# Two accumulation tables in place of one for the expert outputs of a decoder step, and a final stage in two halves

## The reference

```
scores = sigmoid(h @ router_w)                      # 64 experts, 8 chosen for each token
act    = silu(h @ e_gate) * (h @ e_up) * gates      # for each expert, on its tokens
routed = sum over experts of act @ e_down
x      = x + gate2 * (routed + shared)
y      = x * rsqrt(mean(x * x) + EPS) * final_g     # final norm
```

## Time and profile before

| | |
|---|---|
| median of 3 runs | 1003.78 us (1003.36 to 1004.73) |
| time of the profiled execution | 1004.73 us |
| span of the profiled execution | 1003.0 us, first to last instruction |
| mean granted TensorE clock | 0.976 |
| busy share of the span | PE 91%, DVE 47%, ACT 28%, POOL 17% |
| read from HBM, written | 305.79 MB, 25.90 MB |

### The profile page before, as it was taken

One profiled execution on the slowest core, in us unless ns is written; L12 is line 12 of the kernel. 1 busy time (PEld: TensorE's weight loads), 2 busy tenths in 40 slices (PEclk: granted clock), 3 DMA queues, 4 the chain that ended last, 5 costly groups with the idle time before them and its releaser, 6 DMA issues.

```text
span 1003.0 us, 18411 instructions
## 1 busy us (share of the span) xinstructions
PE 916.1 (91%) x6409; PEld 642.9 (64%) x6409; DVE 468.1 (47%) x1217; ACT 276.0 (28%) x491; POOL 172.8 (17%) x177
## 2 busy tenths in 40 slices
PE   2799999999998999999999999999999988889890
PEld 1599999999997986445555555555555445445440
DVE  1557889899968464422333233323223222222124
ACT  3554444443274220012222212221212111111121
POOL 2000000000000001122222222232222222222120
PEclk9899999999999989999999999999999999999995
DMA  9884558878877169679999999999999999999833
GB/s 329 261 250 144 170 174 288 276 252 299 281 260 245 55 234 368 245 270 341 411 397 398 412 394 398 395 403 384 390 393 381 376 374 364 342 367 358 306 97 101
DMA packets 101761, 305.53 MB, mean 305 GB/s; under 512 B 13379, under 2 KB 53379, under 8 KB 76716
## 3 DMA queue, kind: packets, MB, share of 16 engines
q1 hardware_dynamic: 87275, 281.63, 75.1%
q0 software_dynamic: 13936, 21.79, 8.5%
q10 hardware_dynamic: 499, 1.40, 0.4%
HBM read 305.79 MB, written 25.90 MB: 331 GB/s over the span
## 4 chain that ended last, share of the span: by engine, by line
DMA 45%; PE 44%; DVE 5%; issue 4%; ACT 1%; POOLq 0%; SPq 0%; ACTq 0%; POOL 0%; DVEq 0%
DMA y_even<-mT,scatter_row 30%; PE psum L760 26%; DMA wexp<-in_e_up 12%; PE psum L1031 7%; PE psum L764 3%; PE psum L779 2%; PE psum L1059 2%; PE psum L947 1%; DMA bc<-in_norm_g 1%; DMA xn<-h_table,idx 1%; PE psum L1002 1%; DVE wexp_r L1439 1%; DMA mid<-in_c_prompt 0%; DVE x_sb L1990 0%; PE psum L1064 0%
## 5 line engine op out<-in xcount | busy, mean ns | idle before, releaser
L760 PE MATMUL psum<-xn_r,wexp_r 128*128 128x264 f32 x1024 | 191.6, 287 | 2.2 <-DVE wexp_r L1439 2.2
L1033 PE MATMUL psum<-wexp,mid 128*64 128x256 f32 x720 | 175.4, 387 | 11.5 <-DMA wexp<-in_e_up 11.2
L1034 PE MATMUL psum<-wexp,mid 128*64 128x256 f32 x720 | 175.7, 387 | 0.0
L684 POOL DMA_INDIRECT y_even<-mT,scatter_row x64 | 95.1, 1486 | 399.2 <-ACT mT L1359 174.7
L760 PEld LDWEIGHTS psum<-xn_r,wexp_r 128*128 128x128 f32 x1024 | 160.3, 190 | 3.3 <-DVE wexp_r L1439 2.5
L1031 PE MATMUL psum<-wexp,mid 128*128 128x512 f32 x304 | 140.3, 605 | 9.5 <-DMA wexp<-in_e_up 8.7
L760 PE MATMUL psum<-hT_r,wexp_r 128*128 128x264 f32 x512 | 145.6, 284 | 0.0
L1854 DVE SCALAR_TENSOR_TENSOR hT<-psum,gcol,hT 128x256 f32<-128x256 f32 (+1 forms) x64 | 30.6, 478 | 222.5 <-ACT hT L1352 222.5
L1033 PEld LDWEIGHTS psum<-wexp,mid 128*64 128x64 f32 x720 | 92.8, 137 | 51.8 <-issue 17.8
L1862 DVE COPY mT<-psum 128x512 f32<-128x512 f32 (+1 forms) x64 | 43.9, 685 | 175.9 <-DMA y_even<-mT,scatter_row 102.7
L1439 DVE TENSOR_TENSOR wexp_r<-wexp,wexp_r 128x1024 fp32r<-128x1024 f32 x88 | 106.4, 1218 | 22.5 <-ACT wexp_r L1198 22.4
(11 more groups left out here) (285 smaller groups left out, 1008.1 us busy)
## 6 DMA issues: line engine op xcount, KB each, us to landing
wexp<-in_e_gate SPq DMA_DIRECT2D x64, 1024.0 KB, 8.7
wexp<-in_e_up SPq DMA_DIRECT2D x64, 1024.0 KB, 18.9
wexp<-in_e_down SPq DMA_DIRECT2D x64, 1024.0 KB, 19.1
wexp<-in_w_in SPq DMA_DIRECT2D x32, 1024.0 KB, 6.4
mid<-in_ada_w SPq DMA_DIRECT2D x8, 2048.0 KB, 9.8
wexp<-in_ada_w SPq DMA_DIRECT2D x4, 2048.0 KB, 20.5
wexp<-in_w_branch SPq DMA_DIRECT2D x8, 1024.0 KB, 6.1
wexp<-in_w_out SPq DMA_DIRECT2D x4, 1024.0 KB, 5.8
```

What stands on the lines that cost most here:

```text
L684: g.indirect_dma_start(out=y_even, out_offset=bass.IndirectOffsetOnAxis(ap=scatter_row[0:n, j, :].bitcast(mybir.dt.uint32), axis=0), in_=y ...
L760: last = mm(out, a[x], b[y], start=start and x == y == 0, stop=stop and x == 1)
L1033: mm(psum[HALF:CAP, j % 2, 0:FE], x[:, k, 0:HALF], w[:, k, 0], start=(k == 0), stop=(k == KT - 1), tile_position=(0, HALF))
L1034: last = mm(psum[0:HALF, j % 2, 0:FE], x[:, k, 0:HALF], w[:, k, 1], start=(k == 0), stop=(k == KT - 1), tile_position=(0, 0))
```

## The change

Scatters of even places go to `y_even`, those of odd places to `y_odd`, and each table has a semaphore of its own. A scatter waits only for the previous one into the same table, that is for expert e - 2. The waits of `y_out` and `keep_scatter_row` name the same scatters as before, counted by parity. `y_odd` is filled with zeros as well.

The final stage is in two halves. Once the last even scatter (expert 62) has landed, SP loads `y_even`. DVE multiplies and adds it to all three tiles, now ahead of its `extra_passes`. After all scatters and `extra_passes`, `y_odd` is loaded; DVE takes tiles 0 and 1, and POOL takes the 8 rows of tile 2 with the same two operations. The order in which tiles are finished and stored is 0, 1, 2 in place of 2, 0, 1; only the loads of `y_odd` keep 2, 0, 1. POOL waits for both semaphores before its `extra_passes`, and ACT's table load for the root stands ahead of them.

```diff
-        fin_y = wexp[:, 1, 0:3 * D].rearrange("p (t d) -> p t d", t=3)
+        fin_y = wexp[:, 1, :].rearrange("p (a t d) -> p a t d", a=2, t=3)
...
-            for table in (y_even,):
+            for table in (y_even, y_odd):
...
+            sp.wait_ge(S["down_done"], 2 * (NE - 2))
+            sp.wait_ge(scattered[0], 16 * (NE // 2))
+            for t, (t0, n) in enumerate(TILES):
+                sp.dma_start(fin_y[0:n, 0, t], y_even[t0:t0 + n]).then_inc(S["even_load"], 16)
             sp.wait_ge(S["down_done"], 2 * NE)
             extra_passes(sp, extra)
 
             sp.wait_ge(S["moe_done"], 1)
-            sp.wait_ge(S["scattered"], 16 * NE)
-            for t in FINAL_ORDER:
+            for t in (2, 0, 1):
                 t0, n = TILES[t]
-                sp.dma_start(fin_y[0:n, t], y_even[t0:t0 + n]).then_inc(fin_ld[t], 16)
-            for m, t in enumerate(FINAL_ORDER):
-                t0, n = TILES[t]
-                sp.wait_ge(S["fin_ready"], m + 1)
+                sp.dma_start(fin_y[0:n, 1, t], y_odd[t0:t0 + n]).then_inc(fin_ld[t], 16)
+            for t, (t0, n) in enumerate(TILES):
+                sp.wait_ge(S["fin_ready"], t + 1)
...
-            pool.wait_ge(S["tables_zero"], 2 * 16)
+            pool.wait_ge(S["tables_zero"], 4 * 16)
...
-                need(pool, S["scattered"], 16 * e)
+                need(pool, scattered[j % 2], 16 * (2 * i + j // 2))
...
-                g.indirect_dma_start(out=y_even, out_offset=...
+                g.indirect_dma_start(out=(y_even, y_odd)[j % 2], out_offset=...
...
             scatter(NE // UNROLL - 1, UNROLL - 1)
-
-            def all_scattered():
-                pool.wait_ge(S["scattered"], 16 * NE)
+            pool.wait_ge(scattered[0], 16 * (NE // 2))
+            pool.wait_ge(scattered[1], 16 * (NE // 2))
...
-            extra_passes(pool, extra, all_scattered)
+            extra_passes(pool, extra)
             pool.sem_inc(S["moe_done"], 1)
-            all_scattered()
+
+            t, n = 2, NS
+            pool.wait_ge(fin_ld[t], 16)
+            link(g.tensor_tensor(out=fin_y[0:n, 1, t], in0=fin_y[0:n, 1, t], in1=rows_of(3, t, n, 0, D), op=ALU.mult))
+            pool.wait_ge(S["even_taken"], 3)
+            g.tensor_tensor(out=x_sb[0:n, t, :], in0=x_sb[0:n, t, :], in1=fin_y[0:n, 1, t], op=ALU.add).then_inc(S["fin_samples"], 1)
...
-                need(ac, S["scattered"], 16 * (e - 1))
+                need(ac, scattered[j % 2], 16 * (2 * i + j // 2))
...
+            F(sqrt_first[:], epsc[:], ACT.Sqrt)
             extra_passes(ac, extra)
-            F(sqrt_first[:], epsc[:], ACT.Sqrt)
-            for m, t in enumerate(FINAL_ORDER):
-                n = TILES[t][1]
-                ac.wait_ge(S["fin_red"], m + 1)
+            for t, (t0, n) in enumerate(TILES):
+                if t == 2:
+                    ac.wait_ge(S["fin_samples"], 1)
+                else:
+                    ac.wait_ge(S["fin_red"], t + 1)
...
+            ve.wait_ge(S["even_load"], 3 * 16)
+            for t, (t0, n) in enumerate(TILES):
+                link(V.tensor_tensor(fin_y[0:n, 0, t], fin_y[0:n, 0, t], rows_of(3, t, n, 0, D), ALU.mult))
+                V.tensor_tensor(x_sb[0:n, t, :], x_sb[0:n, t, :], fin_y[0:n, 0, t], ALU.add).then_inc(S["even_taken"], 1)
             extra_passes(ve, extra, shift_small)
 
-            for t in FINAL_ORDER:
+            for t in range(2):
                 n = TILES[t][1]
                 ve.wait_ge(fin_ld[t], 16)
-                link(V.tensor_tensor(fin_y[0:n, t], fin_y[0:n, t], rows_of(3, t, n, 0, D), ALU.mult))
-                V.tensor_tensor(x_sb[0:n, t, :], x_sb[0:n, t, :], fin_y[0:n, t], ALU.add).then_inc(S["fin_red"], 1)
+                link(V.tensor_tensor(fin_y[0:n, 1, t], fin_y[0:n, 1, t], rows_of(3, t, n, 0, D), ALU.mult))
+                ve.wait_ge(S["even_taken"], t + 1)
+                V.tensor_tensor(x_sb[0:n, t, :], x_sb[0:n, t, :], fin_y[0:n, 1, t], ALU.add).then_inc(S["fin_red"], 1)
```

More of the change, by code:

```diff
@@ L57 @@
 MIX_ORDER = (2, 0, 1)
-FINAL_ORDER = (2, 0, 1)
 X2_AT = {t: MIX_JOBS.index((t, 1)) + 1 for t in MIX_ORDER}
@@ L336, in bass_decoder_step @@
         gathered = [sem(f"gathered{b}") for b in range(UNROLL)]
+        scattered = [sem(f"scattered{b}") for b in range(2)]
         gu_full = [sem(f"gu_full{s}") for s in range(UNROLL)]
@@ L683, in scatter @@
                 n = rows_used(i, j)
-                g.indirect_dma_start(out=y_even, out_offset=bass.IndirectOffsetOnAxis(ap=scatter_row[0:n, j, :].bitcast(mybir.dt.uint32), axis=0),
+                g.indirect_dma_start(out=(y_even, y_odd)[j % 2], out_offset=bass.IndirectOffsetOnAxis(ap=scatter_row[0:n, j, :].bitcast(mybir.dt.uint32), axis=0),
                                      in_=y_rows[0:n, j % 2, :], in_offset=None,
-                                     bounds_check=last_token, oob_is_err=False, compute_op=ALU.add).then_inc(S["scattered"], 16)
+                                     bounds_check=last_token, oob_is_err=False, compute_op=ALU.add).then_inc(scattered[j % 2], 16)
             await_full(pool, ("h2T", MIX_ORDER[-1], 1))
@@ L720, in extra @@
                 pool.sem_inc(S["dma_may_go"], 1)
-                g.indirect_dma_start(out=y_even, out_offset=bass.IndirectOffsetOnAxis(ap=idx[:, 0, 0:1].bitcast(mybir.dt.uint32), axis=0),
+                g.indirect_dma_start(out=y_odd, out_offset=bass.IndirectOffsetOnAxis(ap=idx[:, 0, 0:1].bitcast(mybir.dt.uint32), axis=0),
                                      in_=y_rows[:, 0, :], in_offset=None,
@@ L1827, in keep_scatter_row @@
                 ve.wait_ge(S["lst_ready"], e + 1)
-                need(ve, S["scattered"], 16 * (e - 3))
+                need(ve, scattered[j % 2], 16 * (2 * i + j // 2 - 1))
                 n = rows_used(i, j)
@@ L1859, in y_out @@
                 ve.wait_ge(S["down_done"], 2 * e + 2)
-                need(ve, S["scattered"], 16 * (e - 1))
+                need(ve, scattered[j % 2], 16 * (2 * i + j // 2))
                 n = rows_used(i, j)
@@ L1975, in extra @@
                 ve.wait_ge(S["x_sc"], 16 * n + 16)
+            ve.wait_ge(S["even_load"], 3 * 16)
+            for t, (t0, n) in enumerate(TILES):
+                link(V.tensor_tensor(fin_y[0:n, 0, t], fin_y[0:n, 0, t], rows_of(3, t, n, 0, D), ALU.mult))
+                V.tensor_tensor(x_sb[0:n, t, :], x_sb[0:n, t, :], fin_y[0:n, 0, t], ALU.add).then_inc(S["even_taken"], 1)
             extra_passes(ve, extra, shift_small)
[L1980 removed]
+            for t in range(2):
                 n = TILES[t][1]
                 ve.wait_ge(fin_ld[t], 16)
[L1983 to L1984 removed]
+                link(V.tensor_tensor(fin_y[0:n, 1, t], fin_y[0:n, 1, t], rows_of(3, t, n, 0, D), ALU.mult))
+                ve.wait_ge(S["even_taken"], t + 1)
+                V.tensor_tensor(x_sb[0:n, t, :], x_sb[0:n, t, :], fin_y[0:n, 1, t], ALU.add).then_inc(S["fin_red"], 1)
             ve.wait_ge(S["ld_fin"], 16)
[L1986 to L1988 removed]
+            for t, (t0, n) in enumerate(TILES):
+                ve.wait_ge(S["fin_sq"], t + 1)
                 link(V.reciprocal(st[0:n, t, 2:3], st[0:n, t, 1:2]))
```

7 lines of the change are left out of this document (2 added, 5 removed).

## The result

The changed kernel takes 1013.40 us (median of 4 runs, 1012.96 to 1013.97), the kernel before on the same chip 1004.06 us (4 runs, 1003.36 to 1004.73): a ratio of 1.0086, 95% interval 1.0064 to 1.0106. The ratio is taken over all fast executions of the changed kernel, 21 with a median of 1012.68 us, and so is a little less than that of the two medians here. So the change costs 9 to 11 us. The direction of the forecast was right. Its size, 3.6 us, was not, and the time lies above the whole range (1009.0).

What follows compares the result with a forecast made beforehand. The prediction took the slowest DMA engine's backlog of weights to bound the loop. With the loop at 0, the end's sum of +0.2 us and POOL's hold of 3.4 gave 1003.78 + 3.6 = 1007.4 us, range 1001.0 to 1009.0.

Steps and rivals of the forecast that it cites:

- Scatters overlap in the loop: Expert loop: free scatters were put at 0, with ends of 3.5 us gained and 1 us lost.
- The sign of the 3.5 us of PE: Loop: PE regains up to 3.5 us from late gathers, taken as no gain; rival of a faster loop, chance 0.20.
- Zeros, 0: Before the loop: filling y_odd takes SP 9.03 us, from 325.5 to 334.6, all covered; cost 0.
- Last scatters: Loop's end: expert 62's scatter goes 0.8 us after its copies, lands 4.53 us later; 63 lands 4.3 us sooner.
- The two of 512 KB take 3.8 us: Final stage: y_even's three loads, issued from 979.25 us, are all there for DVE at 984.0.
- DVE's start: Final stage: DVE begins the even half at 984.0 us.
- head start of 4.5 us: Final stage: DVE starts 4.5 us sooner than before, used up by two more tiles, the branch and one norm.
- POOL holds DVE up: Final stage: DVE stands still for POOL's two instructions, losing 3.4 us; rival that they don't, loop unchanged, chance 0.26.
- ACT's earlier table load changes nothing: Final stage: loading ACT's root table ahead of extra_passes costs nothing, as ACT idles there.
- The branch, 0.4 us on DVE: Final stage: extra_passes, now between DVE's even and odd halves, costs DVE 0.4 us.
- Sum: Whole span: 1003.0 + 0.2 + 3.4 = 1006.6 us; as a time against the median, 1007.4 us.
- the prediction's premise that the slowest engine always has work: Loop: the slowest DMA engine had work waiting from about 560 us on, which sets the last e_up's landing at 939.55.

Runs made afterwards that it cites:

- e2: Changed kernel with POOL's two instructions on the 8 rows of tile 2 moved to DVE; ratio 1.0073 to the kernel before.
- e3: Changed kernel with ACT's first root back behind extra_passes, as in the kernel before; ratio 1.0103 to the kernel before.
- e7: Changed loop with the old end: y_even alone is loaded and added, y_odd left out of the outputs; 1004.31 us, ratio 1.0003 to the kernel before.
- e1: Changed kernel with all scatters serial again, two tables and the new end kept; ratio 1.0064 to the kernel before.
- e5: Changed kernel with an odd expert's scatter waiting for the even one before it; 1008.85 us, ratio 1.0054 to the kernel before.
- e8: Changed kernel, scatters free, with each gather issued ahead of the scatter on POOL; ratio 1.0071 to the kernel before.
- e13: Changed kernel with scatters free only in the loop's first part, serial after the cut at the tenth round; ratio 1.0066 to the kernel before.
- e14: Changed kernel with scatters serial up to the cut at the tenth round and free after it; ratio 1.0084 to the kernel before.
- e4: Kernel before with each gather ahead of the scatter on POOL, scatters still serial into one table; ratio 1.0009 to the kernel before.
- e6: Changed kernel with scatters serial up to expert 61, the samples' odd half on DVE, first root after the branch; ratio 1.0043 to the kernel before.
- e10: e8 with the edits of e2 and e3 added; ratio 1.0030 to the kernel before.
- e11: Changed kernel with an even expert's scatter waiting for the odd one before it; ratio 1.0087 to the kernel before.
- e12: The changed kernel itself, measured once more; ratio 1.0113 to the kernel before.
- e9: e5 with the edits of e2 and e3 added; ratio 1.0027 to the kernel before.

## Why the prediction was wrong

Point by point, by its own steps, for the profiled execution.

- **"Scatters overlap in the loop ... I take 0 ... and 1 us lost."** This step failed. The term put at 0 cost 3.6 us (2.0 in the second profile of the same kernel, 3.2, 3.2 and 4.2 in e2, e3 and e7 with the same loop). "Moved bytes are the same" is true but for the zeros, yet equal bytes did not take equal time: at 939 us the changed kernel stood 1.06 MB behind, with ten packets or fewer under way for 15.5 us in place of 6.1. The bound of 1 us was one scatter's latency, and looked at the last place only. e1 and e5 show that the loss comes with free scatters, e8 that the order of gathers belongs to it. Against the kernel before it falls in the round from 762.6 to 803.1 us, where the time to landing comes to its limit; that it belongs to the scatters behind about 764 us stands on the profiles of e13 and e14.
- **The sign of the 3.5 us of PE.** Right that they are no gain in the times: e4 takes them back without touching the tables and stays at 1.0009 (0.9996 to 1.0022), though its profile is 2.0 us shorter.
- **Zeros, 0.** Right. The second pair occupied SP for 4.3 us, not 9.0, with more than 27 us to spare.
- **Last scatters.** The mechanism was right: 62 goes 0.9 us after its copies end, and lands 4.32 us later (4.53 taken).
- **"The two of 512 KB take 3.8 us ... 980.05 + 3.9 = 984.0."** Too short: DVE waits for all three loads, the last takes 5.26 us, and from landing to DVE's start it is 6.2 us (982.65 to 988.86) where 4.85 were summed. This adds 1.35. The runs show by what. From SP's first load to DVE's start it is 6.2 us here, 5.9 to 6.3 in the other runs in which expert 63's scatter goes ahead of the loads (e2, e3, e6, e10, e11, e12, e14), and 6.8 in e8. Where that scatter waits for 62's and goes 0.9 us behind them, it is 5.0 to 5.1 (e1, e5, e9, e13). So the scatter ahead of the loads costs 1.1 us.
- **DVE's start.** 984.0 foretold, 988.86 measured: 4.9 us = 3.6 of the loop, 1.35 of the load, and 0.1 less between. So the head start of 4.5 us over the kernel before (988.52) was gone.
- **POOL holds DVE up, "2 x 1.9 - 0.4 = 3.4 us".** The mechanism was right, and shown by e2; the size was near. DVE lost 3.24 - 1.23 = 2.0 us twice, 4.0 in all. POOL's first row is 2.67 long, but of that it stood 0.5 for DVE's row of 988.86; from the end of that row to its own it is 2.2 us (990.09 to 992.29), and 2.2 again the second time (999.29 to 1001.48). In e12, e3 and e1 it is 2.2 to 2.3. The 0.4 that I took off for a head start was not there: the branch gave no pause, and DVE's next product had started 0.2 us before POOL's addition, which waited for it in its turn.
- **"ACT's earlier table load changes nothing."** Wrong in mechanism, small in size: ACT loads the table three times, the last between the first square and the first root, 1.28 us. e3 shows 0.3 to 0.4 us of path, and nothing that the times can tell. **The branch, 0.4 us on DVE,** cost about nothing (the even half ends at 998.13, the odd one begins at 998.06 in the records). The two cancel.
- **Sum.** From DVE's start to the end 22.6 us were foretold and 23.0 came. Of the 5.3 us by which the span misses the forecast (1011.9 - 1006.6), 4.9 lie ahead of DVE's start.

The Trainium skill (SBUF — State Buffer, SBUF: two separate sides, on the port pair that VectorE and GpSimd share) says that such instructions shut each other out for their whole length, the one that started first going on. The rows agree: DVE's row ends 1.1 us after POOL's, which is its own working time. The estimate of 2.25 us from the Trainium skill (GPSIMD Engine Reference, Elementwise) fits the 2.2 us measured better than the 1.9 that I took, and the loss of 4.1 us estimated from it stands against 4.0 measured.

What stays open is why scatters in the order scatter, gather lead to longer waits on one expert in four and to a later end of the loop, when the order gather, scatter does not. The chain "long wait, lower clock, slot held longer, SP late, engines dry" is what the changed kernel's trace shows, but it is not shown to be the cause: e8 has the same chain and loses nothing by the end, and e9, with ten packets or fewer for 14.3 us, has one of the fastest loops. The steps and the packets show that half of the engines run dry while the other half has weights to bring. So the prediction's premise that the slowest engine always has work isn't refuted. What that engine carries more, or carries more slowly, in the changed kernel is not shown, because the trace doesn't say which engine moved a packet.

## What to carry to other kernels

A queue that is "30 us behind" is not a promise that its engines are busy; it can be one engine that is behind: look at the share in windows of a few us behind each long wait before costing a change of traffic at nothing. And count what was moved from the start, not in a window alone: the window here showed 1.44 MB missing, and 1.06 MB were. Taking a wait out of a stream of small transfers is worth only what the path gets from it; in the best version here the end began 5.9 us sooner and took 6.3 us longer, because DVE had to add a second table without a pause. And give a second engine a share of elementwise work only where the first one has a pause: two inputs from SBUF on both, and each stands for the other's whole length.

## What the hardware showed beyond the forecast

- DVE's 128x1024 addition took 3.24 to 3.35 us beside POOL's 8x1024 product or addition, and 1.22 to 1.23 alone. POOL's row is 2.33 to 3.21 us long, 2.2 to 2.3 of it after DVE's row before had ended.
- Three loads of ACT's table (1.28 us each) for one function, when its first use stands ahead of a branch that may not be taken; one when it stands behind.
- The clock: behind waits of PE of 3.9, 4.5 and 4.9 us the granted clock fell to the lower level and the up product took 5.39, 6.36 and 6.21 us; behind a wait of 0.6 us it took 3.70. Behind 2.6 us it took 5.39 in the changed kernel (at 823.69) and 3.70 before (at 860.41).
- A scatter issued ahead of the end's three loads made them land 1.1 us later.
- One free pair of scatters in two left the loop as fast as none (e5) or nearly (e11); both free cost 2.0 to 4.2 us against the kernel before (976.1 against 978.1 to 980.3).
- A load's time to landing was its slowest share's: of 16 semaphore steps of one 1 MB load, eight came after 6.6 to 8.2 us and the last after 31.1 (issued at 766.4). Early in the loop all 16 came after 9.6 to 11.8 us.
